# Places for weights by age, sums of squares in four column groups, and other counts of half rows, in a two-layer decoder step on one core

## What is computed

```python
def rmsnorm(x, g):
    y = xf * lax.rsqrt(jnp.mean(xf * xf, axis=-1, keepdims=True) + NORM_EPS)
    return (y * g).astype(x.dtype)
def adaln_pre(x, m, g):
    return rmsnorm(x, g) * (1 + m[:, 1][:, None]) + m[:, 0][:, None]
def adaln_post(x, y, m, g, res_w):
    return x + res_w * m[:, 2][:, None] * rmsnorm(y, g)
def swiglu(h, w_in, w_out):
    gt, up = jnp.split(h @ w_in, 2, axis=-1)
    return (jax.nn.silu(gt) * up) @ w_out
```

## Time and profile before

| | us |
|---|---|
| Median of three timed runs | 2614.08 |
| The profiled execution | 2613.64 |
| Its span in the trace | 2612.0 |
| TensorE busy | 2501.7 |
| VectorE busy | 1191.5 |
| ScalarE busy | 992.8 |

### The profile page before, as it was taken

How to read it: one execution, slowest core, us unless ns; L and a number is a source line. 1 busy time by engine, 2 the same in 40 slices (tenths; PEclk the granted TensorE clock), 3 DMA queues, 4 the chain that set the end, 5 groups by cost and what they waited for, 6 DMA issues and landing times.

```text
span 2612.0 us, 43828 instructions
## 1 busy us (share of the span) xinstructions
PE 2501.7 (96%) x18904; PEld 2242.9 (86%) x18904; DVE 1191.5 (46%) x1646; ACT 992.8 (38%) x1376; POOL 125.1 (5%) x268
## 2 busy tenths in 40 slices
PE   5999999999979999999999999899999999999997
PEld 4999999964678999899899999876676899899997
DVE  3333336634456333246533236655554546533335
ACT  4322235526555322235522235432222445522233
POOL 0000000112200000000000000001222100000000
PEclk9999999999989999999999999999999999999999
DMA  6555245893534654475555335544445445543244
GB/s 252 170 154 153 72 133 169 267 225 116 164 117 147 189 156 148 144 244 159 174 163 155 110 124 173 182 149 149 158 157 160 136 142 165 158 134 95 73 154 144
DMA packets 116866, 407.14 MB, mean 156 GB/s; under 512 B 23098, under 2 KB 23226, under 8 KB 116290
## 3 DMA queue, kind: packets, MB, share of 16 engines
q1 hardware_dynamic: 81154, 282.65, 34.9%
q10 hardware_dynamic: 19584, 69.21, 8.5%
q0 software_dynamic: 15936, 52.47, 6.2%
HBM read 380.87 MB, written 23.41 MB: 155 GB/s over the span
## 4 chain that ended last, share of the span: by engine, by line
PE 84%; DVE 7%; ACT 5%; issue 2%; DMA 2%; SPq 0%; ACTq 0%; POOL 0%; POOLq 0%; DVEq 0%
PE PS L1731 66%; PE PS L1187 3%; DVE WL L1951 3%; PE PS L1691 3%; ACT WH L1811 2%; PE PS L1140 1%; PE PS L1749 1%; PE PS L1135 1%; PE PS L1094 1%; ACT Y L1855 1%; PE PS L613 1%; PE PS L1125 1%; PE PS L1106 1%; PE PS L545 1%; ACT L1831 1%
## 5 line engine op out<-in xcount | busy, mean ns | idle before, releaser
L1951 DVE TENSOR_TENSOR WL<-RAW,WH 128x1024 fp32r<-128x1024 f32 (+1 forms) x468 | 617.4, 1320 | 809.0 <-ACT WH L1811 807.8
L1731 PE MATMUL PS<-HH,WH 128*128 128x260 f32 x3584 | 840.6, 290 | 51.4 <-DVE HL L2038 37.6
L1731 PE MATMUL PS<-HH,WL 128*128 128x260 f32 x3584 | 818.7, 284 | 0.0
L1731 PE MATMUL PS<-HL,WH 128*128 128x260 f32 x3520 | 802.5, 284 | 0.0
L1811 ACT ACTIVATE WH<-RAW 128x1024 fp32r<-128x1024 f32 (+1 forms) x468 | 528.5, 1130 | 423.8 <-PE PS L1731 305.4
L1731 PEld LDWEIGHTS PS<-HH,WH 128*128 128x128 f32 x3584 | 595.3, 190 | 106.0 <-issue 89.2
L1731 PEld LDWEIGHTS PS<-HH,WL 128*128 128x128 f32 x3584 | 597.1, 190 | 0.0
L1731 PEld LDWEIGHTS PS<-HL,WH 128*128 128x128 f32 x3520 | 585.3, 190 | 0.8 <-issue 0.2
L1731 PE MATMUL PS<-GH,WH 128*128 128x260 f32 x1408 | 376.6, 288 | 12.7 <-DVE WL L1951 12.7
L1731 PE MATMUL PS<-GL,WH 128*128 128x260 f32 x1408 | 372.3, 285 | 0.0
L1731 PE MATMUL PS<-GH,WL 128*128 128x260 f32 x1408 | 371.8, 285 | 0.0
(11 more groups left out here) (289 smaller groups left out, 2238.7 us busy)
## 6 DMA issues: line engine op xcount, KB each, us to landing
RAW<-in_w_in SPq DMA_DIRECT2D x224, 512.0 KB, 3.6
RAW<-in_w_out SPq DMA_DIRECT2D x112, 704.0 KB, 4.1
AW<-in_w_ada ACTq DMA_DIRECT2D x128, 512.0 KB, 3.6
RAW<-in_w_odd SPq DMA_DIRECT2D x60, 512.0 KB, 3.6
RAW<-in_w_even SPq DMA_DIRECT2D x28, 512.0 KB, 4.2
RAW<-in_w_odout SPq DMA_DIRECT2D x28, 512.0 KB, 3.6
AFIRST<-in_w_ada SPq DMA_DIRECT2D x4, 2048.0 KB, 19.8
RAW<-in_w_evout SPq DMA_DIRECT2D x16, 512.0 KB, 3.9
```

Source lines behind the costliest of these rows:

```text
L1731: last = nc.tensor.matmul(ps[:, x, 0:HT], w[:, at_ + k * P:at_ + (k + 1) * P], src[k0 + k][:, x, :], start=(begin and t == 0), stop=(end a ...
L1951: nc.vector.tensor_tensor(WL[:, at_:at_ + w], RAW[:, from_:from_ + w], WH[:, at_:at_ + w].bitcast(F32), ALU.subtract).then_inc(lo_done, 1)
```

## The change

Four things change together.

- Places (`oldest_first`): each unit takes, of the places allowed to it, the one whose last user lies longest back. The last W8 unit before a W11 stage may take only the first or the third place. Worked out from the code, the first unit of each W11 stage needed the unit right before it to be done, and now the one before that; in3[0] needed the unit right before it, and now the one two earlier than that.
- Sums of squares: the eight matmuls of a norm, each with 128 equal output columns, become eight with 32 output columns, in four column groups, so that four partial sums stand in four groups of 32 partitions. ScalarE copies them to NT (`gather_sums`), and one more matmul with ones (the fold) adds them up, 32-fold, at the step of "root".
- in1, in2 and in3 run 16 half rows ahead instead of 14; out0, out1, out2, odout and out3 share one output block instead of two. That makes 16 more steps (468 to 484), each with a load and a split of its own, and the same matmuls.
- The step tables: in TIGHT and ROWS12 the second square and the sums come up to a step earlier, in TAIL all from "root" on comes two steps later, and in ROWS16 one step later, with the second half starting two steps later.

The core of the diff:

```diff
-AHEAD = {"in0": 6, "evin": 12, "in1": 14, "in2": 14, "odin": 12, "in3": 14}
-SHARED = {"out0": 2, "evout": 0, "out1": 2, "out2": 2, "odout": 2, "out3": 2}
+AHEAD = {"in0": 6, "evin": 12, "in1": 16, "in2": 16, "odin": 12, "in3": 16}
+SHARED = {"out0": 1, "evout": 0, "out1": 1, "out2": 1, "odout": 1, "out3": 1}
...
-FOLLOWS = {"evout": len(STEPS["evin"])}
...
-    return (i % 2) * W11 if WIDTH[name] == W11 else ((i + FOLLOWS.get(name, 0)) % 3) * W8
...
-    return i % 2 if name == "odin" and i >= AHEAD[name] else (i + FOLLOWS.get(name, 0)) % 3
...
-    users = [q for q in range(max(0, p - 6), p) if at(q) < hi and lo < at(q) + WIDTH[STAGE_OF[q]]]
...
+def oldest_first(places):
+
+    at, free, used = [], [], []
+    for p in range(TOTAL):
+        w = WIDTH[STAGE_OF[p]]
+        best = None
+        for n, lo in enumerate(places(p)):
+            last = max([q + 1 for q, l, h in used if l < lo + w and lo < h], default=0)
+            if best is None or last < best[0]:
+                best = (last, n, lo)
+        used = used[-6:] + [(p, best[2], best[2] + w)]
+        free.append(best[0])
+        at.append((best[1], best[2]))
+    return at, free
...
+def weight_places(p):
+    if WIDTH[STAGE_OF[p]] == W11:
+        return (0, W11)
+    before_wide = p + 1 < TOTAL and WIDTH[STAGE_OF[p + 1]] == W11
+    return (0, 2 * W8) if before_wide else (0, W8, 2 * W8)
...
     if WIDTH[name] == W11:
-        return i % 2
-    return i % 2 if name == "odin" and i >= AHEAD[name] else (i + FOLLOWS.get(name, 0)) % 3
+        return (0, W11)
+    kept = name == "odin" and i >= AHEAD[name] or name == "odout" and i < 2
+    return (0, W8) if kept else (0, W8, 2 * W8)
...
+WEIGHT_PLACE, WEIGHT_FREE = oldest_first(weight_places)
+RAW_PLACE, RAW_FREE = oldest_first(raw_places)
...
-TIGHT = dict(zip(PIECES, (0, 1, 1, 2, 2, 3, 4, 4, 3, 5, 5, 6, 6, 7, 6, 7, 8, 9)))
...
+TIGHT = dict(zip(PIECES, (0, 1, 1, 2, 2, 3, 3, 3, 3, 4, 5, 6, 6, 7, 6, 7, 8, 9)))
...
-TAIL = dict(zip(PIECES, (0, 1, 1, 2, 2, 2, 3, 3, 4, 5, 5, 6, 6, 7, 7, 8, 9, 10)))
...
+TAIL = dict(zip(PIECES, (0, 1, 1, 2, 2, 3, 4, 4, 4, 6, 7, 8, 8, 9, 9, 10, 11, 12)))
...
-ROWS12 = dict(zip(PIECES, (0, 1, 1, 2, 2, 3, 4, 4, 4, 6, 6, 7, 7, 8, 8, 9, 10, 11)))
-ROWS14 = dict(zip(PIECES, (0, 1, 2, 3, 3, 4, 5, 5, 5, 7, 7, 8, 9, 10, 10, 11, 12, 13)))
...
+ROWS12 = dict(zip(PIECES, (0, 1, 1, 2, 2, 3, 3, 3, 4, 5, 6, 7, 7, 8, 8, 9, 10, 11)))
+ROWS16 = dict(zip(PIECES, (0, 1, 2, 3, 3, 4, 5, 5, 5, 7, 8, 9, 10, 11, 11, 12, 13, 14)))
...
-        return [(name, i) for i in range(2 * AHEAD[name] - (4 if name in ("in1", "in2") else 0), len(STEPS[name]))]
+        return [(name, i) for i in range(2 * AHEAD[name] - (6 if name in ("in1", "in2") else 0), len(STEPS[name]))]
...
                             buf = (SQ, SG)[n % 2]
                             for e in range(2):
-                                last = nc.tensor.matmul(ST[:, x, 0:HT], ONES[:], buf[:, e, x, :], start=(n + e == 0),
-                                                        stop=(n == 3 and e == 1))
+                                j = CG * (2 * (n % 2) + e)
+                                last = nc.tensor.matmul(ST[j:j + CG, x, 0:HT], ONES[:, 0:CG], buf[:, e, x, :],
+                                                        start=(g == 0), stop=(g == 1), tile_position=(0, j))
                             last.then_inc(sq_used[x], 1)
+                if b < 6 and k == SLOTS[b, x]["root"]:
+                    pe.wait_ge(part_ok[x], b + 1)
+                    nc.tensor.matmul(ST[:, x, 0:HT], ONES[:], NT[:, x, :], start=True, stop=True).then_inc(folded[x], 1)
...
-                stats(0, x, 5)
+                for k in range(3, 6):
+                    stats(0, x, k)
...
+            def gather_sums(b, x):
+
+                act.wait_ge(sq_used[x], 4 * b + 4)
+                nc.scalar.activation(NT[:, x, :], ST[:, x, 0:HT], ACT.Copy).then_inc(part_ok[x], 1)
...
+                if k == at_["sum1"]:
+                    gather_sums(b, x)
...
+                if x == 0:
+                    act.wait_ge(sa_ok, 1)
+                gather_sums(0, x)
...
-            def variance(x):
-                nc.vector.tensor_scalar(VAR[:, x], ST[:, x, 0:HT], 1.0 / DM, EPS, ALU.mult, ALU.add).then_inc(var_ok, 1)
+            def variance(x, n):
+                nc.vector.tensor_scalar(VAR[:, x], ST[:, x, 0:HT], 1.0 / n, EPS, ALU.mult, ALU.add).then_inc(var_ok, 1)
...
                 if k == at_["root"]:
-                    dve.wait_ge(sq_used[x], 4 * b + 4)
-                    variance(x)
+                    dve.wait_ge(folded[x], b + 1)
+                    variance(x, CG * DM)
```

More of the change, by code:

```diff
@@ L84, with raw_places @@
 STAGE_OF = [name for name in ROWS for _ in STEPS[name]]
-FOLLOWS = {"evout": len(STEPS["evin"])}
-def weight_at(p):
-    name = STAGE_OF[p]
-    i = p - POS[name]
-    return (i % 2) * W11 if WIDTH[name] == W11 else ((i + FOLLOWS.get(name, 0)) % 3) * W8
-def raw_slot(p):
+def oldest_first(places):
[16 more added lines that the diff above has]
+    return (0, 2 * W8) if before_wide else (0, W8, 2 * W8)
+def raw_places(p):
     name = STAGE_OF[p]
@@ L99, in raw_slot, with weight_at @@
     if WIDTH[name] == W11:
-        return i % 2
-    return i % 2 if name == "odin" and i >= AHEAD[name] else (i + FOLLOWS.get(name, 0)) % 3
-def raw_at(p):
-    return raw_slot(p) * WIDTH[STAGE_OF[p]]
-def last_user(p, at):
-    lo, hi = at(p), at(p) + WIDTH[STAGE_OF[p]]
-    users = [q for q in range(max(0, p - 6), p) if at(q) < hi and lo < at(q) + WIDTH[STAGE_OF[q]]]
-    return users[-1] + 1 if users else 0
-WEIGHT_FREE = [last_user(p, weight_at) for p in range(TOTAL)]
-RAW_FREE = [last_user(p, raw_at) for p in range(TOTAL)]
+        return (0, W11)
[3 more added lines that the diff above has]
+RAW_PLACE, RAW_FREE = oldest_first(raw_places)
+def weight_at(p):
+    return WEIGHT_PLACE[p][1]
+def raw_slot(p):
+    return RAW_PLACE[p][0]
+def raw_at(p):
+    return RAW_PLACE[p][1]
 RAW_COUNT = [16 * sum(raw_slot(q) == raw_slot(p) for q in range(p + 1)) for p in range(TOTAL)]
@@ L144 @@
           "refine_x", "norm0", "norm1", "shift0", "shift1", "split0", "split1")
-TIGHT = dict(zip(PIECES, (0, 1, 1, 2, 2, 3, 4, 4, 3, 5, 5, 6, 6, 7, 6, 7, 8, 9)))
-TAIL = dict(zip(PIECES, (0, 1, 1, 2, 2, 2, 3, 3, 4, 5, 5, 6, 6, 7, 7, 8, 9, 10)))
-ROWS12 = dict(zip(PIECES, (0, 1, 1, 2, 2, 3, 4, 4, 4, 6, 6, 7, 7, 8, 8, 9, 10, 11)))
-ROWS14 = dict(zip(PIECES, (0, 1, 2, 3, 3, 4, 5, 5, 5, 7, 7, 8, 9, 10, 10, 11, 12, 13)))
-SLOTS = {(0, 0): TIGHT, (0, 1): TIGHT, (1, 0): TAIL, (1, 1): ROWS12, (2, 0): TIGHT, (2, 1): ROWS14, (3, 0): TAIL,
-         (3, 1): ROWS14, (4, 0): TAIL, (4, 1): ROWS12, (5, 0): TAIL, (5, 1): ROWS14, (6, 0): TIGHT, (6, 1): TIGHT}
+TIGHT = dict(zip(PIECES, (0, 1, 1, 2, 2, 3, 3, 3, 3, 4, 5, 6, 6, 7, 6, 7, 8, 9)))
+TAIL = dict(zip(PIECES, (0, 1, 1, 2, 2, 3, 4, 4, 4, 6, 7, 8, 8, 9, 9, 10, 11, 12)))
+ROWS12 = dict(zip(PIECES, (0, 1, 1, 2, 2, 3, 3, 3, 4, 5, 6, 7, 7, 8, 8, 9, 10, 11)))
+ROWS16 = dict(zip(PIECES, (0, 1, 2, 3, 3, 4, 5, 5, 5, 7, 8, 9, 10, 11, 11, 12, 13, 14)))
+SLOTS = {(0, 0): TIGHT, (0, 1): TIGHT, (1, 0): TAIL, (1, 1): ROWS12, (2, 0): TIGHT, (2, 1): ROWS16, (3, 0): TAIL,
+         (3, 1): ROWS16, (4, 0): TAIL, (4, 1): ROWS12, (5, 0): TAIL, (5, 1): ROWS16, (6, 0): TIGHT, (6, 1): TIGHT}
 def root_index(b, x, pre):
@@ L440, in decoder_step @@
         y_act = sem("y_act"); y_dve = sem("y_dve"); acc_step = sem("acc_step")
+        part_ok = [sem("part_ok_a"), sem("part_ok_b")]; folded = [sem("folded_a"), sem("folded_b")]
         var_ok = sem("var_ok"); ln_ok = sem("ln_ok"); exp_ok = sem("exp_ok"); newton = sem("newton")
@@ L1786, in _ @@
             for x in range(2):
-                stats(0, x, 3)
-                stats(0, x, 5)
+                for k in range(3, 6):
+                    stats(0, x, k)
             for c in range(16):
@@ L2046, in boundary @@
                     dve.wait_ge(sum_done[x], b)
-                    variance(x)
+                    variance(x, DM)
                 if b and k == at_["refine_y"]:
```

## The result

The changed kernel takes 2571.65 us (median of 4 runs, 2569.1 to 2573.8), the kernel before beside it 2613.89 us (median of 4). The ratio, estimated from all timed executions, is 0.9841, 95% interval 0.9827 to 0.9856 (the two medians alone give 0.9838): 42 us or 1.6% faster. The prediction was 2567.0 us, 2551 to 2585. The profiled execution took 2569.1 us, 44.5 less than that of before, where 47.2 were forecast.

What follows compares the result with a forecast made beforehand. TensorE, busy 2501.7 of 2612.0 us, was taken as the bound. The terms 20.0 + 4.5 + 12.6 + 10.2 + 0 + 1.6 - 1.7 = 47.2 us came off 2613.6, giving about 2567 us, range 2551 to 2585.

Steps and rivals of the forecast that it cites:

- Places: Starts of out0 to out3 and in3: waits for a place and the lower clock behind them go, 24.5 us.
- the slower rival: W11 half steps: loads landing too late make the kernel slower, 2620 us at a landing of 5.9; chance 3%.
- Sums: Sums of squares on TensorE: column groups save 1.5 us a norm, 15 us for ten norms on the path.
- Norm's chain: Half-row stretches: in2, in1 with evout, and in3 with odout gain 12.6 us, cheaper sums included, clock apart.
- The walk: The three in-order queues worked through piece by piece to forecast waits; said to overstate by a tenth or two.
- The clock in the half-row stretches: in1, in2, in3 after the turn to the second half: no lower clock, 3.4 us each, 10.2 us.
- a 30% rival: Half-row stretches: clock stays low, 10.2 us not won, odin may lose some 3 more; 2578 to 2581 us; 30%.
- 1.0 and 1.3 us of new waits: evin and odin: new waits as large as the gain of the out stage before each; net 0.
- The second wait for squares: evout to in1: a second wait of 2.4 us for squares appears and could lower the clock again.
- the 1.7 set aside for its clock: evout to in1: 1.7 us subtracted for a lower clock after the new wait for squares.
- The start: Kernel's start, where the sums lie on the chain: at most 1.6 us come of them.

Runs made afterwards that it cites:

- places alone: Kernel before with only the new choice of places for RAW, WH and WL; steps, tables and sums as before: 2590.69 us, ratio 0.992.
- the kernel with places and groups and the old tables: Kernel before with new places and column groups, but 14 half rows, two shared output blocks and old step tables: 2589.23 us, ratio 0.9921.
- wide sums: Kernel after with sums of squares put back to eight matmuls of 128 output columns, without copy and fold: 2580.13 us, ratio 0.9885.
- The tables of their own: Kernel after with separate new step tables for evin and odin instead of ROWS12: 2558.75 us, ratio 0.9796.
- groups alone: Kernel before with only the narrow sums in four column groups, the copy and the fold; places, steps and tables as before: 2610.22 us, ratio 1.0001.
- the kernel with a new ROWS16: Kernel after with only the step table of in1, in2 and in3 changed (root at 6, both norms at 9, second shift at 14): 2561.89 us, ratio 0.9812.
- the table for evout: Kernel after with one table changed: evout's norm of x = 0 gets its pieces earlier than in TIGHT: 2556.84 us, ratio 0.9791.
- kernel with all tables: Kernel after with new tables for evout, in1 to in3, evin and odin, and y's first-half write held until all weights are split: 2533.78 us, ratio 0.9702.

## Why the prediction was right, and where it was off

**Places: right.** In the kernel after TensorE waits for no weights at any of the five starts, and the clock is 1.00 behind them. The stages that hold only this and a norm's first half, out0, out1 and out2, are within 0.5 us of the forecast, and places alone gave 24.6 where 24.5 were summed. Two loads more in a row at W11, the slower rival, did nothing: the landing stayed at 4.1 us. out3 is the exception, 1.5 short. Its last units wait 0.95 us at [24] and 0.41 at [26] for WL. ScalarE's timeline there, kernel after:

```profile
2519.39 1.38 ACT L1835 ACTIVATE WH<-RAW 128x1408 fp32r<-128x1408 f32 x1 [3.17 <-DMA RAW<-in_w_out]
2524.45 1.38 ACT L1835 ACTIVATE WH<-RAW 128x1408 fp32r<-128x1408 f32 x1 [3.04 <-DMA RAW<-in_w_out]
```

Transfers issued between 2510 and 2545 us, kernel after (KB each, median us to landing):

```profile
RAW<-in_w_out SPq DMA_DIRECT2D x8, 704.0 KB, 4.9
out_y_t<-X POOLq DMA_DIRECT2D x2, 520.0 KB, 5.1
```

The write of y's first half runs beside the last loads, which land in 4.9 us there (median; 4.1 in the 50 us before). This is the mechanism of the slower rival on a small scale. With the write held back the loads land in 4.1, no such wait is left, and out3 took 127.3 us, where the kernels with the new steps and tables and without that edit took 128.0 to 129.4. But that the write is the cause is likely and not shown: in the kernel with places and groups and the old tables the write runs beside the last loads too, they land in 4.1, nothing waits, and out3 takes the same 127.3.

**Sums: the price right, the place not.** A group costs 0.80 to 0.85 (0.76 taken), the fold 0.43 to 0.45 (0.5 taken): 1.4 a norm saved (1.5 taken). But "for ten norms on the path 15 us" held only in part. Taking the groups out costs 11.1 us by the traces, 3.5 of them in evout by another way, and shortens odin by 2.3. In in2, steps [5] to [11] take 24.9 us with wide sums and 23.9 with groups: 1.0 and not 1.4 is gained, since TensorE, sooner done, waits 1.39 us for what comes next (0.31, 0.58 and 0.50) where it waits 0.93 with wide sums.

**Norm's chain: right.** in2 gained 5.7 us (6.9 forecast, clock included; 1.1 of the 1.2 between are the clock's, see below). The waits at [14], [15] and [16] were to be 1.5, 0.7 and 1.3; they are 1.24, 0.31 and 1.07, in all three stages alike. The walk overstated, as it had for the old tables. Those at [6], [8] and [11], walked at 0.4 to 0.7, are 0.31, 0.58 and 0.50.

**The clock in the half-row stretches: right, against a 30% rival, but priced too high.** No stretch at half rate is left in in1 past its start, in in2 or in in3; the window from 1244 to 1254 us holds a wait of 1.07 and ran at 1.00. The 10.2 us for it were too many, though. The prediction took half of 6.9 us in each of the three stages, but the second wait of the turn lies within that stretch and was counted on its own as well. Windows of the kernel before, in2 and in3 (in1 is in the earlier trace rows):

```profile
1263.40:1270.30 6.90, 4.53 (x22) 4.30 (x21) 2.71 (x3) 3.46 (x5) 0.00 (x0) 0.51 0.48 151
2239.60:2246.50 6.90, 4.80 (x23) 4.50 (x22) 2.89 (x4) 3.24 (x5) 0.00 (x0) 0.51 0.51 151
```

TensorE was busy for 5.30, 4.53 and 4.80 us there, and half of that is 7.3. The prediction had reckoned so for out0, with 5.99 busy of 6.8. These 2.9 us, the largest of its errors downwards, explain 1.1 of the 1.2 that in2 is short and 1.0 of the 1.5 in odout and in3; in1's 0.8 is covered by what evout gave.

**evin and odin: mis-sized.** Of "1.0 and 1.3 us of new waits" the first came out in time: evin is 1.2 us longer, with 1.0 forecast, though its new waits are 0.38 and 1.67, 2.05 in all, less the cheaper sums. In odin two stand on either side of the second sums, at the end of [5] and before [6]. TensorE's timeline, kernel after:

```profile
1630.70 0.63 PE L1770 MATMUL PS<-SQ,ONES 128*32 128x260 f32 x4 [1.90 <-ACT SQ L1871]
1633.43 0.58 PE L1207 MATMUL PS<-WH,HH 128*128 128x512 f32 x1 [1.57 <-DVE WL L1985]
```

With 0.85 at odin[5] that is 4.3 us where the kernel before had one wait of 1.04, so 3.3 new and not 1.3, and the 3.4 us behind them ran at 0.50, which costs 1.7; a shorter wait at [10] and the cheaper sums take some of it back. ROWS12 has scale, add and square of the second group all in step 3, and TensorE reached the sums before ScalarE had the squares. The kernel with wide sums and the same tables has the wait for squares (1.85) but neither the 0.85 nor the 1.57 for weights, and its odin takes 450.4: the overrun comes of the table and the groups together. The tables of their own took 7.2 us out of odin.

**evout and in1: 4.1 us more than forecast.** The second wait for squares, 2.02 us where it was 0.41 before, is there, but the 1.7 set aside for its clock wasn't paid: the stretch at half rate there (3.4 us from 739.4) had its twin before (744.6). The rest is a wait of another kind. TensorE's timeline, the adaLN blocks ahead of evout's first unit, kernel after:

```profile
692.12 0.64 PE L1711 MATMUL PS<-AW,CSP 128*32 128x256 f32 x8 [0.19 <-DMA AW<-in_w_ada]
693.36 0.64 PE L1711 MATMUL PS<-AW,CSP 128*32 128x256 f32 x8 [0.60 <-DMA AW<-in_w_ada]
```

In the kernel before the two waits were 0.37 and 2.00, and 3.4 us at half rate followed: 1.6 and 1.7, 3.3 us that the sum did not hold. With the 1.7 not paid that is 5.0; less the 0.8 by which in1's clock gave less than forecast it is 4.2, near the 4.1. In all 11 kernels of this study the total is 2.4 or 2.5 us with wide sums (three kernels) and 0.8 to 1.2 with groups (eight). Two loads are issued back to back there, at the same distance in each, and in the kernel before the slowest of that stretch landed in 5.8 us, in groups alone in 5.0. Why the form of the sums, which are not in this stretch, should go with that is open; no run here separates it. A second execution of the same code also differs: in the kernel with a new ROWS16 evout, with the attention ahead of it, took 1.4 us more than in the kernel after.

**The start: in part luck.** in0 ended 1.7 us sooner, with 1.6 forecast as the most. But the first product starts at 42.8 to 43.3 us in the eight kernels with groups and at 43.6, 44.1 and 44.4 in the three with wide sums, of which the kernel before is the latest. On the means the groups are worth 1.0 us there.

So the sum was 2.7 us from the profiled execution, with errors of both signs: +4.1 in evout and in1, -1.5 in odin, -1.5 in out3, -1.2 in in2, -1.5 in odout and in3, and -0.9 in small ones. That they nearly cancel is luck: the one upwards is mostly a wait for transfers that the prediction did not know of. The rest of the distance from 2567.0 to the median of 2571.65 is that the profiled execution lies 2.55 us below its own median.

## What to carry over

Cheaper work on the bottleneck engine pays only if what feeds it stands a step ahead: here the column groups alone gave nothing, because a copy that TensorE had to wait for came with them. Cost the new wait together with the saving, at the place in the order where it falls. And a wait that looks like an amount of work (12 us before in1[0]) may be an order of pieces: walk the queues with another order before calling it fixed.

## What the runs showed of the hardware

A group of narrow matmuls costs TensorE 0.3 to 0.4 us besides its own time, once a group, whether four or eight stand in it (0.84 and 1.21 us). Half rate does not need a long wait: with the table for evout, behind the 2.01 us of in1[0], with 1.15 and 1.26 in the 13 us before, TensorE ran at 0.50 for 3.4 us. Window of the kernel with all tables, columns as above:

```profile
747.60:751.00 3.40, 3.32 (x15) 3.35 (x16) 3.40 (x5) 2.15 (x4) 0.00 (x0) 0.50 0.43 139
751.00:761.30 10.30, 10.05 (x82) 9.78 (x81) 7.86 (x12) 6.40 (x11) 0.00 (x0) 1.00 0.50 151
```

And the wait of 2.65 us before out1 in the kernel before left it at 1.00: the length of the wait alone doesn't tell it.
